# Recurrence scores from crossed and summed keys, a separate buffer for the first head, and four final sums on TensorE

## The reference

```
for l in range(2):
    x = x + 0.5 * rmsnorm(swiglu(rmsnorm(x, g[0]), ...), g[1])
    h = rmsnorm(x, g[2])
    m = mla(h, ...) if l == 0 else hgrn2(h, ...)
    x = x + rmsnorm(m, g[3])
    x = x + 0.5 * rmsnorm(swiglu(rmsnorm(x, g[4]), ...), g[5])
```

```
S_t = diag(f_t) S_{t-1} + k_t outer v_t ;  o_t = S_t^T q_t
```

## Time and profile before

| | before |
|---|---|
| time, median of 3 runs | 2115.07 us (2113.66 to 2117.83) |
| profiled execution, time | 2110.53 us |
| profiled execution, span | 2108.8 us |
| TensorE busy | 2066.9 us, 98% |
| VectorE busy | 897.2 us, 43% |
| ScalarE busy | 688.7 us, 33% |
| GpSimd busy | 664.7 us, 32% |
| mean granted clock of TensorE | 0.99 |

### The profile page before, as it was taken

One profiled execution on the slowest core, in us unless ns is written; L12 is line 12 of the kernel. 1 busy time (PEld: TensorE's weight loads), 2 busy tenths in 40 slices (PEclk: granted clock), 3 DMA queues, 4 the chain that ended last, 5 costly groups with the idle time before them and its releaser, 6 DMA issues.

```text
span 2108.8 us, 31342 instructions
## 1 busy us (share of the span) xinstructions
PE 2066.9 (98%) x12670; PEld 1696.2 (80%) x12670; DVE 897.2 (43%) x1223; ACT 688.7 (33%) x930; POOL 664.7 (32%) x286
## 2 busy tenths in 40 slices
PE   9999999989999999999999999999999999999997
PEld 7888888767878888887888888878888778888885
DVE  5433421668464333015433311565755765333213
ACT  4222232445342222224222222463544443222221
POOL 3444444130214444442444444200000013444442
PEclk9999999999999999999999999999999999999998
DMA  4223233210122222332222233212211122222332
GB/s 150 97 92 99 88 99 97 86 50 1 52 89 90 92 97 95 95 99 90 85 94 99 87 102 93 96 62 71 72 62 62 51 70 85 95 99 90 95 101 75
DMA packets 51643, 179.61 MB, mean 85 GB/s; under 512 B 5728, under 2 KB 5984, under 8 KB 51552
## 3 DMA queue, kind: packets, MB, share of 16 engines
q1 hardware_dynamic: 51552, 178.30, 26.0%
HBM read 176.18 MB, written 2.10 MB: 85 GB/s over the span
## 4 chain that ended last, share of the span: by engine, by line
PE 92%; DVE 5%; ACT 2%; issue 1%; DMA 0%; SPq 0%; DVEq 0%; ACTq 0%
PE psum L555 27%; PE psum L557 26%; PE psum L556 26%; PE psum L816 1%; PE psum L792 1%; PE psum L920 1%; PE psum L673 1%; PE psum L668 1%; PE psum L667 1%; DVE xt L1615 1%; PE psum L805 1%; PE psum L652 1%; ACT xg_hi L1232 1%; DVE xg_lo L1621 1%; DVE t_a L1610 0%
## 5 line engine op out<-in xcount | busy, mean ns | idle before, releaser
L505 POOL TENSOR_TENSOR w_lo<-raw,w_hi 128x1024 fp32r<-128x1024 f32 (+1 forms) x282 | 664.5, 2357 | 1413.5 <-ACT w_hi L1189 1413.4
L555 PE MATMUL psum<-xg_hi,w_hi 128*128 128x512 f32 x1758 | 699.3, 398 | 11.6 <-DVE xg_lo L1917 4.7
L557 PE MATMUL psum<-xg_hi,w_lo 128*128 128x512 f32 x1758 | 691.0, 393 | 0.0
L556 PE MATMUL psum<-xg_lo,w_hi 128*128 128x512 f32 x1758 | 689.4, 392 | 0.0
L1189 ACT ACTIVATE w_hi<-raw 128x1024 fp32r<-128x1024 f32 (+1 forms) x339 | 350.8, 1037 | 841.2 <-DMA raw<-w_up 462.0
L555 PEld LDWEIGHTS psum<-xg_hi,w_hi 128*128 128x128 f32 x1758 | 331.7, 189 | 86.2 <-DVE t_a L1673 6.0
L557 PEld LDWEIGHTS psum<-xg_hi,w_lo 128*128 128x128 f32 x1758 | 331.7, 189 | 74.5
L556 PEld LDWEIGHTS psum<-xg_lo,w_hi 128*128 128x128 f32 x1758 | 332.1, 189 | 70.2
L555 PE MATMUL psum<-hid_hi,w_hi 128*128 128x512 f32 x704 | 273.9, 389 | 0.0
L557 PE MATMUL psum<-hid_hi,w_lo 128*128 128x512 f32 x704 | 273.9, 389 | 0.0
L556 PE MATMUL psum<-hid_lo,w_hi 128*128 128x512 f32 x704 | 273.9, 389 | 0.0
(11 more groups left out here) (199 smaller groups left out, 1562.0 us busy)
## 6 DMA issues: line engine op xcount, KB each, us to landing
raw<-w_up SPq DMA_DIRECT2D x176, 512.0 KB, 3.3
raw<-w_down SPq DMA_DIRECT2D x64, 512.0 KB, 3.5
raw<-w_hgrn SPq DMA_DIRECT2D x48, 512.0 KB, 3.3
raw<-w_down SPq DMA_DIRECT2D x32, 384.0 KB, 3.1
raw<-w_mla SPq DMA_DIRECT2D x19, 512.0 KB, 3.3
xt<-x_t SPq DMA_DIRECT2D x8, 256.0 KB, 6.9
out<-xt SPq DMA_DIRECT2D x8, 256.0 KB, 2.0
sq<-positions SPq DMA_DIRECT2D x1, 256.0 KB, 9.4
```

What stands on the lines that cost most here:

```text
L505: pool.tensor_tensor(w_lo[slot][:, 0:n], raw[slot][:, 0:n], w_hi[slot][:, 0:n].bitcast(F32), ALU.subtract).then_inc(w_ready, 1)
L555: first = pe.matmul(ps, w_hi[slot][:, at:at + n], hi, start=start, stop=False)
L556: pe.matmul(ps, w_hi[slot][:, at:at + n], lo, start=False, stop=False)
L557: return first, pe.matmul(ps, w_lo[slot][:, at:at + n], hi, start=False, stop=stop)
```

## The change

1. **Crossed keys.** A buffer `k_crossed` gets, for level `m`, the keys of direction 0 in the first half of every block and those of direction 1 in the second (`cross_keys` on ScalarE, a copy of 128x1024 for each of 20 levels). `masked` makes one product of 32x32 per cell, with queries read in the same crossed way, in place of two with 16 queries each. `update` multiplies the keys first and the queries after, with a semaphore of its own for the keys.
2. **Summed keys.** `first_level` on VectorE first adds the keys of both directions (`keys_sum`, 128x1024, four times), and `diagonal` makes one product per cell in place of two.
3. **Opening.** The third projection moves ahead of `turn_values(0, 0)` and `diagonal(0)`, and `project_first` waits for the bank it uses alone.
4. **First head.** The first head's parts go to `o_first`, in the memory of `sq`; `o_hi(0)` no longer waits for the last projection. ScalarE later copies them into `xg_hi` and `xg_lo` for the last three groups. `cross_keys(n, 4)`, `(n, 8)` and `(n, 16)` stand among ScalarE's steps of the last quarter.
5. **Final sums.** For blocks 0 to 3 VectorE makes one step (`y` times gain times `WIDE`), TensorE adds `xt` and `y` in PSUM by two fp32 products with the identity, and ScalarE copies the sum to `xt`. Blocks 4 to 7 stay as they were, after those.

```diff
 def masked(n, m, closing=False):
     ps = open_scores()
     pe.wait_ge(level_ready, LEVELS_UP * n + m.bit_length())
+    pe.wait_ge(keys_crossed, N_MASKS * n + m.bit_length())
     for c in range(CELLS):
         for g in range(P // SUB):
-            out_c = of_cell(ps, c, g).rearrange("p (b two m) -> p b two m", two=2, m=m)
-            for d in range(2):
-                queries = q_lev[n % 2][:, 1 - d, cell(c, g)]
-                queries = queries.rearrange("p (b two m) -> p b two m", two=2, m=m)
-                last = pe.matmul(out_c[:, :, 1 - d, :], k_lev[n % 2][:, d, cell(c, g)],
-                                 queries[:, :, 1 - d, :], start=True, stop=True)
+            last = pe.matmul(of_cell(ps, c, g), k_crossed[:, cell(c, g)],
+                             crossed_cell(q_lev[n % 2], cell(c, g), m), start=True, stop=True)
...
 def diagonal(n):
-    pe.wait_ge(gate_ready, Z_TILES * (n + 1))
+    pe.wait_ge(keys_summed, n + 1)
...
-            for d in range(2):
-                last = pe.matmul(of_cell(ps, c, g), k_lev[n % 2][:, d, cell(c, g)], q_raw[:, cell(c, g)],
-                                 start=d == 0, stop=d == 1)
+            last = pe.matmul(of_cell(ps, c, g), keys_sum[:, cell(c, g)], q_raw[:, cell(c, g)],
+                             start=True, stop=True)
...
-                project(by_dve=False)
-                project(by_dve=False)
+                project_first(0, by_dve=False)
+                project_first(1, by_dve=False)
+                project_first(2)
                 turn_values(0, 0)
                 diagonal(0)
-                project()
                 turn_values(0, 1)
                 masked(0, 1)
-                project()
+                project_first(3)
...
+def cross_keys(n, m):
+    if m > 1:
+        act.wait_ge(keys_ready, (LEVELS_UP - 1) * n + m.bit_length() - 1)
+    else:
+        act.wait_ge(gate_ready, Z_TILES * (n + 1))
+        if n:
+            act.wait_ge(score_done, SCORES * n)
+    act.activation(k_crossed[:, :].rearrange("p (b two m) -> p b two m", two=2, m=m),
+                   crossed(k_lev[n % 2], m), ACT.Copy).then_inc(keys_crossed, 1)
...
                 hi_part()
+                cross_keys(n, 2)
                 output_gate(n, 0)
                 hi_part()
-                act.wait_ge(drained, out_of_psum.count + 1)
                 o_hi(0)
                 take_root([(0, CELLS, P)], TAIL_BANKS[0])
+                act.wait_ge(drained, out_of_psum.count + 1)
+                o_hi(1)
+                cross_keys(n, 4)
                 output_gate(n, 1)
-                o_hi(1)
                 o_hi(2)
                 o_hi(3)
+                cross_keys(n, 8)
...
+            carry(0, SUMMED_BY_PE[0])
             pe.wait_ge(recip_made, recips.next())
             widen()
+            carry(1, SUMMED_BY_PE[1])
+            add(0, SUMMED_BY_PE[0])
+            for n, j in enumerate(SUMMED_BY_PE[2:], 2):
+                carry(n, j)
+                add(n - 1, SUMMED_BY_PE[n - 1])
+            add(len(SUMMED_BY_PE) - 1, SUMMED_BY_PE[-1])
...
-            for j in range(KB):
+            for j in SUMMED_BY_PE:
+                dve.scalar_tensor_tensor(y[:, j, :], y[:, j, :], gains_of(last, j), psum[:, WIDE, :],
+                                         ALU.mult, ALU.mult).then_inc(y_scaled, 1)
+            for j in range(len(SUMMED_BY_PE), KB):
                 normed(j)
```

More of the change, by code:

```diff
@@ L878, in project, with project_first @@
                     group(xg_hi, xg_lo, by_dve=by_dve)
+                def project_first(i, by_dve=True):
+                    slot = open_tile(by_dve)
+                    pe.wait_ge(drained, first_group + i + 1)
+                    group_into(next_bank(LONG_RING), slot, xg_hi, xg_lo)
                 def open_scores():
@@ L1038, in output_step @@
                         for c in range(h + 1) if begins[g] == h else (h,):
-                            first, last = mm3(banks[g], (tiles[g], c * P, P), xg_hi[:, c, :], xg_lo[:, c, :],
-                                              c == 0, c == HEADS - 1)
+                            o_hi = xg_hi[:, c, :] if c else o_first[:, 0, :]
+                            o_lo = xg_lo[:, c, :] if c else o_first[:, 1, :]
+                            first, last = mm3(banks[g], (tiles[g], c * P, P), o_hi, o_lo, c == 0, c == HEADS - 1)
                             if c == g == 0:
@@ L1119, in fifth_step @@
                 def fifth_step(h):
-                    first, last = mm3(fifth, (fifth_slot, h * P, P), xg_hi[:, h, :], xg_lo[:, h, :],
-                                      h == 0, h == HEADS - 1)
+                    o_hi = xg_hi[:, h, :] if h else o_first[:, 0, :]
+                    o_lo = xg_lo[:, h, :] if h else o_first[:, 1, :]
+                    first, last = mm3(fifth, (fifth_slot, h * P, P), o_hi, o_lo, h == 0, h == HEADS - 1)
                     if h == HEADS - 1:
@@ L1520, in hgrn @@
                 o_hi(5)
+                cross_keys(n, 16)
+                act.wait_ge(chunk_ready, 5 * KB + MLA_LORA + 1)
+                act.activation(xg_hi[:, 0, :], o_first[:, 0, :].bitcast(F32), ACT.Copy)
+                act.activation(xg_lo[:, 0, :], o_first[:, 1, :].bitcast(F32), ACT.Copy).then_inc(o_moved, 1)
                 nearest_out(n)
```

73 lines of the change are left out of this document (58 added, 15 removed).

## The result

| | before | changed |
|---|---|---|
| time, median | 2114.36 us (4 runs, 2111.88 to 2117.83) | 2094.43 us (4 runs, 2094.33 to 2094.48) |
| profiled execution, span | 2108.8 us | 2092.7 us |
| TensorE busy | 2066.9 us | 2057.3 us |
| VectorE busy | 897.2 us | 922.3 us |
| ScalarE busy | 688.7 us | 714.5 us |

The ratio is 0.9905 with a 95% interval of 0.9887 to 0.9922: 19.9 us less. The prediction was 2094.

A forecast was written before the change was run, and what follows sets the result against it. TensorE, busy 2066.9 of 2108.8 us, was taken to bound the kernel. Savings of 10.7 + 2.9 + 1.2 + 3.4 + 2.8 = 21.0 us, off a median of 2115.07, gave 2094 us, range 2088 to 2100.

The forecast's parts named there:

- Part 1, masked levels: TensorE's score steps: 64 records in place of 128 save 0.67 us a level, 10.7 us for 16 levels.
- Part 2, diagonals: TensorE's diagonal in each of four quarters: 1.41 us becomes 0.69, together 2.9 us.
- Part 3, copies at 0: ScalarE's 20 crossed copies between levels end before TensorE returns from its projection, 1.7 us or more left: cost 0.
- Part 4, opening: Start of the recurrence: the third projection covers TensorE's 1.53 us wait, less new waits; about 1.2 us.
- the fall of the clock at 1560: TensorE at 0.50 though never idle, behind statistics and level 2; up to 1.7 us each if such falls go.
- Part 5, last quarter: Statistics to 64 level: 22.7 us in place of 26.07, 3.4 us earlier, with levels 2 to 16 included.
- Because VectorE leads, the clock matters little: Last quarter: even at half clock `output_step(0)` takes 4.1 us and still ends before level 4 at 8.0.
- half of part 5 or less: Rival: last quarter or steady slots give half; 3 to 5 us less gain, 2097 to 2099; 9 in 100.
- Part 6, final sums: End of the run: four blocks' sums on TensorE shorten VectorE's closing work; 2.8 us if the clock holds.
- the rival: End of the run: final products at half clock, ending 2.1 us later than before; 2099 us; 9 in 100.
- The rival of the 25 ns floor: Masked levels: at 25 ns a matmul a level would save 1.6 us; 2077 us; 1 in 100.
- the forecast for the span: Whole profiled execution: span 2108.8 us becomes 2087.8 by taking off the 21.0 us sum.

The follow-up runs named there:

- experiment 2: `masked_two`: the changed kernel with masked levels as two products per cell, 128 records, crossed copies kept but unread; median 2106.64 us, ratio 0.9959.
- experiment 5: The changed kernel with every crossed copy made twice on ScalarE, the second signalling; median 2095.53 us, ratio 0.9912.
- experiment 12: The changed kernel with idle products in the last quarter's waits, five final sums on TensorE and `o_low(2)` ahead of the split; median 2091.37 us, ratio 0.9903.
- open_back: The changed kernel with the third projection behind the first diagonal again, as before the change; median 2096.58 us, ratio 0.9915.
- diag_two: The changed kernel with the diagonal as two accumulated products per cell, the sum of keys still made; median 2101.99 us, ratio 0.993.
- fill_all: The changed kernel with idle fp32 products of 256 columns in TensorE's waits of the last quarter; median 2091.94 us, ratio 0.9896.
- experiment 1: The kernel before, no edit, timed and profiled a second time; median 2113.53 us, ratio 0.9999.
- first_back: The changed kernel with the first head's parts in `xg_hi` and `xg_lo` again, behind the last eviction, without the later copy; median 2095.53 us, ratio 0.9913.
- the fifth sum: The changed kernel with five final sums on TensorE in place of four; median 2098.14 us, ratio 0.9928.

## Why the prediction was right

The sum was 21.0 us, the medians moved by 19.9 (16.5 to 23.9 by the interval), and the number came to 0.4 us. That closeness is in part luck. From the recurrence's entry to the end of the span, where the whole change lies, the change is 20.2 us shorter than the first profile of before and 17.5 shorter than the second. So the sum was 1 to 3.5 us too large, and the median of before had moved down by 0.7 since the forecast. The mechanism is right: TensorE's time in the cells goes with the number of records, and the copies are hidden. By its steps:

- **Part 1, masked levels**: 0.67 forecast, 0.66 read (1.36 to 0.70), and 0.12 less for each level 1. Without the change of the products 12.2 us are lost (experiment 2; its profile has stops of open cause besides). That cost follows the number of records and not of columns was right, also at the crossed reads but for level 1. The changed rows are again at 10.9 ns a record. The floor of about 25 ns from start to start (the Trainium skill, "TensorE: Matmul & The Clock Gate", Part 1) does not show in them; by it one level alone would take an estimated 1.6 us.
- **Part 2, diagonals**: 0.72 each, 1.41 to 0.70 in the rows.
- **Part 3, copies at 0**: right. No level of quarters 0 to 2 waits, and 1.1 us more on each changes next to nothing (experiment 5). But the slack was 0.9 us at the tightest place and not 1.7: there the copy stood behind a gate and a high part in ScalarE's FIFO. The copies take 1.18 us on average, 1.55 at level 1, and not 1.04.
- **Part 4, opening**: from the widening to level 2, 33.86 us before and 31.30 after, 2.56 less. Forecast: 0.72 + 0.67 + 1.2 = 2.6. The leftover waits were over-sized by a little, level 1 under-sized.
- **From level 2 of quarter 0 to the last statistics**: 238.50 to 224.96, 13.5 less. By parts 1 and 2 it is 12.2 less 0.4 for three levels 1; the rest is the fall of the clock at 1560, not in the sum. The second profile of before, without that fall, has 236.93, 12.0 more than the change.
- **Part 5, last quarter**: 3.4 forecast, 2.2 measured, and 1.5 against the second profile of before (25.33). This is the term that was mis-sized. `output_step(0)` at 3.27, level 4 at 8.07, `output_step(1)` at 9.35 came as worked out (3.2, 8.0, 9.3). The step that failed is `o_low(2)`, put at 14.9: `output_step(2)` starts at 15.65. The sum let the split ahead of it start at once, but VectorE waits there 0.60 us for ScalarE, which makes the copy of level 8 first and the high part that the split needs after it. With `o_low(2)` ahead of the split the step starts at 14.84 and the 64 level at 23.12 (experiment 12). The rest is TensorE's own work behind it, 8.2 us where 7.6 were added up (4.1 + 0.7 + 2.8; the sum printed as 22.7 makes 22.5).
- **"Because VectorE leads, the clock matters little"** held up to `output_step(2)`: with the clock falling on `output_step(0)` (`open_back`, `diag_two`), on `output_step(1)` (the change) or nowhere (`fill_all`), that step starts 15.6 to 15.7 us behind the statistics. It does not hold behind it, where TensorE leads: a fall on `output_step(2)` put the 64 level at 25.4 to 25.5 in place of 23.9.
- **Behind the 64 level** nothing was counted; 0.5 us was lost against the first profile of before and 1.1 against the second. With the 2.2 this leaves half of part 5 or less, which the prediction had among its rivals.
- **Part 6, final sums**: 2.8 forecast, 2.5 at the end less 0.15 ahead of the widening, 2.4. The clock held. VectorE's share was under-sized (3.5 us and not 3.0); left out was that the stores queue behind the fourth sum, which took 1.0 of it back. Two numbers of this part do not add up: the copy of the fourth sum, by its own terms at 2101.2, is 2.3 us and not 2.8 ahead of 2103.5, and the rival puts the widening at 2095.6 where the row has 2093.59. Neither enters the 2.8.
- **The rival of the 25 ns floor** is given 2077, which takes 38 us alone from the median and leaves parts 4 to 6 out.
- **The median against the profile**: I put the 21.0 under a median 4.5 us above the profiled execution. The profiled execution of before was a favourable one, by its start: 40.34 against 46.02 in experiment 1. The four runs of the change lie within 0.15 us of each other, and their profile, with a start of 45.42, is one of them. So the forecast for the span (2087.8, measured 2092.7) was 5 us too low by the start alone, while that for the median was not touched by it.

## What to carry to other kernels

Price a small product by the step from start to start, in the form it will have (columns of the array, columns moved), from the nearest row; two half-filled products that can be made one save one of them. When a copy on another engine buys them, work out when it ends and when the first engine comes back: with 0.9 us to spare at the tightest place it was free, with one copy more it cost about 1 us, all but 0.3 of TensorE's waits for it in the last quarter, and with two more it cost most of the gain. Look also at what stands ahead of the copy, and behind it, in its engine's queue. Moving work to an idle engine stops paying where its results join an in-order queue behind it, as the fifth sum did in the store queue and, for 1.0 us, the fourth.

## What the runs showed of the hardware

- Products in cells of 32 array columns went at 10.6 to 11.0 ns a record, for 16 and for 32 moved columns alike; level 1, whose reads alternate between two rows at each column, took 2 ns a record more (0.82 us for 64).
- A wait of TensorE of 1.4 to 1.7 us next to one-column or narrow products was followed by a stretch at half clock in most profiles; idle products in the waits kept it at 1.00 and gave 2.5 us back. In the recurrence it also fell twice with TensorE never idle, each time behind statistics and a level of 128 records: at 1560 in one of two profiles of before, and at 1482 in `masked_two`.
- The start of the run varied by 5 us (40.3 to 46.0), the stretch from there to the recurrence's entry, identical in all variants of the change, by 4.8 us (1323.75 in `first_back` to 1328.53 in `fill_all`). The clock falls at other places and for other lengths in each. The change's four runs agreed within 0.15 us, those of the kernels that differ from it by a few lines spread by 2 to 7.
- Four stores of 256 KB issued by SyncE within 2.0 us ended 3.4 us behind the last block; one every 1.5 us ended 2.4 us behind it.
